# Half of the first block's down projection put off behind the convolution's input products, with its hidden values and split weights kept in DRAM

## The reference

```
# first layer, at its end
h = rms_norm(x, norm_ffn_g)
gp = dwconv_centered(h @ w_ffn_gate, conv_w, conv_b)      # 3 taps over the positions, 2816 channels
x = x + (silu(gp) * (h @ w_ffn_up)) @ w_ffn_down          # the down projection
# second layer, at its start
h = rms_norm_2(x, mix_norm)
a, g = split(h @ a_w_in + a_b_in, 2)                      # two products of 1024 x 1024
u = a * sigmoid(g)
y = causal depthwise convolution of u with 31 taps + conv_b
y = silu(layer_norm(y))                                   # mean and variance over the channels
x = x + y @ a_w_out + a_b_out
x = x + square(relu(rms_norm_2(x) @ w1)) @ w2
```

## Time and profile before

| | |
|---|---|
| median of 3 runs | 3270.68 us (3269.22 to 3271.22) |
| the profiled execution | 3276.46 us, its span 3274.6 us |
| PE busy | 3152.3 us, 96% of the span |
| DVE, ACT, POOL busy | 2012.7, 1067.3, 374.1 us (61%, 33%, 11%) |
| DMA | 288.80 MB, mean 88 GB/s |
| mean granted TensorE clock | 0.982 of full speed |

### The profile page before, as it was taken

How to read it: one execution, slowest core, us unless ns; L and a number is a source line. 1 busy time by engine, 2 the same in 40 slices (tenths; PEclk the granted TensorE clock), 3 DMA queues, 4 the chain that set the end, 5 groups by cost and what they waited for, 6 DMA issues and landing times.

```text
span 3274.6 us, 54823 instructions
## 1 busy us (share of the span) xinstructions
PE 3152.3 (96%) x23414; PEld 2544.0 (78%) x23414; DVE 2012.7 (61%) x3047; ACT 1067.3 (33%) x1528; POOL 374.1 (11%) x354
## 2 busy tenths in 40 slices
PE   8998998899999998999999999999999999999999
PEld 7787886777777777778888888887746888788887
DVE  6665554466766775545444444469979988755544
ACT  5222334445444443222111111132253333433332
POOL 0222441000000000301000000020000000110000
PEclk9999999799999999999999999999999999999999
DMA  3343665122222223421111111111101222223222
GB/s 148 126 135 99 214 213 186 54 75 81 69 86 75 82 81 116 148 90 52 39 52 52 52 42 49 52 39 52 39 13 52 103 91 103 90 90 126 94 91 76
DMA packets 93537, 288.80 MB, mean 88 GB/s; under 512 B 12400, under 2 KB 38640, under 8 KB 72816
## 3 DMA queue, kind: packets, MB, share of 16 engines
q1 hardware_dynamic: 79104, 233.39, 21.1%
q0 software_dynamic: 14192, 51.91, 4.6%
HBM read 228.64 MB, written 56.62 MB: 87 GB/s over the span
## 4 chain that ended last, share of the span: by engine, by line
PE 82%; DVE 10%; ACT 2%; issue 2%; DMA 2%; POOL 1%; SPq 1%; DVEq 0%; ACTq 0%; POOLq 0%
PE ps L2441 24%; PE ps L307 21%; PE ps L489 7%; PE ps L1744 4%; PE ps L2247 3%; PE ps L2603 2%; PE ps L1755 2%; DVE Yh L2630 2%; PE ps L1767 2%; PE ps L2063 1%; PE ps L1387 1%; PE ps L1404 1%; PE ps L1008 1%; PE ps L1398 1%; DVE wlo L287 1%
## 5 line engine op out<-in xcount | busy, mean ns | idle before, releaser
L2441 PE MATMUL ps<-Hh,whi 128*128 128x512 f32 x1600 | 497.6, 392 | 1.3 <-DVE uA L2562 0.7
L283 ACT ACTIVATE whi<-raw 128x2048 fp32r<-128x2048 f32 x139 | 265.5, 1910 | 522.2 <-PE ps L307 296.1
L287 DVE TENSOR_TENSOR wlo<-raw,whi 128x2048 fp32r<-128x2048 f32 x139 | 321.2, 2311 | 95.0 <-ACT whi L283 94.6
L2441 PEld LDWEIGHTS ps<-Hh,whi 128*128 128x128 f32 x1600 | 300.0, 188 | 70.5 <-issue 5.3
L2441 PE MATMUL ps<-Hh,wlo 128*128 128x512 f32 x800 | 311.4, 389 | 0.0
L307 PE MATMUL ps<-Hhi,wlo 128*128 128x512 f32 x672 | 206.9, 389 | 0.0
L307 PE MATMUL ps<-Hlo,whi 128*128 128x512 f32 x672 | 206.9, 389 | 0.0
L307 PE MATMUL ps<-Hhi,whi 128*128 128x512 f32 x672 | 206.8, 389 | 0.0
L2441 PE MATMUL ps<-aHh,whi 128*128 128x512 f32 x512 | 199.5, 390 | 2.7 <-DVE wlo L287 2.5
L2441 PE MATMUL ps<-aLh,whi 128*128 128x512 f32 x512 | 199.2, 389 | 0.0
L2441 PE MATMUL ps<-aHh,wlo 128*128 128x512 f32 x512 | 199.2, 389 | 0.0
(11 more groups left out here) (389 smaller groups left out, 6181.8 us busy)
## 6 DMA issues: line engine op xcount, KB each, us to landing
raw<-in_panels SPq DMA_DIRECT2D x139, 1024.0 KB, 4.8
rwf<-F POOLq DMA_DIRECT2D x16, 1280.0 KB, 6.6
L<-rwf SPq DMA_DIRECT2D x16, 1024.0 KB, 5.0
L<-rwf SPq DMA_DIRECT2D x64, 256.0 KB, 3.5
gts<-so POOLq DMA_DIRECT2D x16, 512.0 KB, 3.5
gl<-gts SPq DMA_DIRECT2D x32, 256.0 KB, 3.6
rwt<-so POOLq DMA_DIRECT2D x15, 512.0 KB, 2.9
qkd<-XTs POOLq DMA_DIRECT2D x16, 384.0 KB, 4.0
```

Of the source, the lines that this page charges most:

```text
L283: e.activation(whi[i % 2][:, :], raw_of(i)[:, :], AF.Copy).then_inc(*a_hi.up(i))
L287: e.tensor_tensor(wlo[i % 2][:, :], raw_of(i)[:, :], whi[i % 2][:, :].bitcast(F32), OP.subtract).then_inc(*v_lo.up(i))
L2441: m = e.matmul(ap, W[wi][:, kc, n0:n0 + 128], mov[mi][:, kc, :], start=x == 0 and q == 0, stop=x == len(kcs) - 1 and q == 2)
```

## The change

**Feed-forward layer.** Only half 0 of the down projection stays in its place (`down_pe`, now 48 matmuls a block, and DVE 8 additions instead of 16). Half 1's rounded part and rest of the hidden values go into `aX` and `aY`, and POOL stores them to DRAM (`hid_pool`, tensors `hdh`, `hdl`). Meanwhile 20 panels are split ahead, the convolution's 8 input panels and 12 panels of the down weights in another cut (`fe`): in 40 pieces of 128 x 1024. POOL loads a piece, ACT rounds it, DVE subtracts, and POOL stores both parts (tensors `sph`, `spl`). There is a single set of buffers for a piece; `sraw` and `slo` are the same memory. So the next load waits until both stores of the piece before have landed. Two pieces go with each channel up to channel 19.

**Convolution.** PE's order is now: half 0's input products, the put-off down projection of half 1 (`rest_pe`, 528 matmuls), half 1's input products, then half 1's taps, `co` and so on. SP loads the split panels back (`pre_sp`, 2 MB each, three sets of buffers) and the hidden values (`hb_sp`). All 248 taps of half 0 are DVE's (`ahead_dve`), two channel tiles in alternation. Half 0's mean and variance sums are formed by POOL (seven additions each), with one product with ones each. POOL's 8 small copies of the 30 positions at the seam (`tail_pool`) go to DVE (`edge_dve`).

```diff
+    def save_load(e, s):
+        i, cols_ = part_s(s)
+        if s:
+            e.wait_ge(*d_ss.by("save", s - 1, "lo"))
+        e.dma_start(sraw[:, :], A["panels"][PIX[SAVED[i]]][:, cols_]).then_inc(*d_sl.up("save", s, "in"))
+    def save_act(e, s):
+        e.wait_ge(*d_sl.by("save", s, "in"))
+        e.activation(shi[:, :], sraw[:, :], AF.Copy).then_inc(*a_ff.up("save", s))
+    def save_dve(e, s):
+        e.wait_ge(*a_ff.by("save", s))
+        e.tensor_tensor(slo[:, :], sraw[:, :], shi[:, :].bitcast(F32), OP.subtract).then_inc(*v_ff.up("save", s))
+    def save_store(e, s):
+        i, cols_ = part_s(s)
+        e.wait_ge(*v_ff.by("save", s))
+        e.dma_start(sph[i][:, cols_], shi[:, :].bitcast(F32)).then_inc(*d_ss.up("save", s, "hi"))
+        e.dma_start(spl[i][:, cols_], slo[:, :].bitcast(F32)).then_inc(*d_ss.up("save", s, "lo"))
...
     def ffn_act(e):
         for blk in range(11):
             for k in range(2):
                 ch = 2 * blk + k
+                if 2 * ch < PIECES_S:
+                    save_act(e, 2 * ch)
                 e.wait_ge(*v_ff.by("c2", ch))
                 e.activation(cv, cv, AF.Silu).then_inc(*a_ff.up("silu", ch))
...
+                if 2 * ch + 1 < PIECES_S:
+                    save_act(e, 2 * ch + 1)
...
     def ffn_pool(e):
         e.wait_ge(*v_h.by(1, "rs"))
+        save_load(e, 0)
         for ch in range(22):
             e.wait_ge(*a_ff.by("silu", ch))
             e.tensor_tensor(cv, cv, rs2, OP.mult).then_inc(*g_ff.up(ch))
+            if ch and ch % 2 == 0:
+                hid_pool(e, ch // 2 - 1)
+            for s in (2 * ch, 2 * ch + 1):
+                if s < PIECES_S:
+                    save_store(e, s)
+                if s + 1 < PIECES_S:
+                    save_load(e, s + 1)
+        hid_pool(e, 10)
...
     def late_pe(e):
         first_pe(e, 0)
+        for ch in range(2, 8):
+            in_pe(e, 0, ch)
+        for g in range(3):
+            rest_pe(e, g)
         first_pe(e, 1)
-        taps_pe(e, 0, 0)
-        for ch in range(2, 8):
-            in_pe(e, ch)
-            taps_pe(e, 0, ch - 1)
-        taps_pe(e, 0, 7)
-        taps_pe(e, 1, 0)
-        mean_pe(e, 0)
-        taps_pe(e, 1, 1)
-        taps_pe(e, 1, 2)
-        var_pe(e, 0)
-        for ch in range(3, 6):
+        for ch in range(2, 6):
+            in_pe(e, 1, ch)
+        added_pe(e, "mu", 0, sy[0])
+        in_pe(e, 1, 6)
+        added_pe(e, "var", 0, sy[1])
+        in_pe(e, 1, 7)
+        for ch in range(4):
             taps_pe(e, 1, ch)
         co_pe(e, 0)
-        taps_pe(e, 1, 6)
+        taps_pe(e, 1, 4)
         last_pe(e, 0)
-        taps_pe(e, 1, 7)
+        for ch in range(5, 8):
+            taps_pe(e, 1, ch)
```

More of the change, by code:

```diff
@@ L2289, in build @@
     rs2 = sb("rs2", 198, [128, S])[:, :]
-    aH = [sb(f"aH{i}", 152 + 16 * i, [128, 2, S], F32R) for i in range(2)]
-    aL = [sb(f"aL{i}", 160 + 16 * i, [128, 2, S], F32R) for i in range(2)]
+    aH = [sb(f"aH{i}", 152 + 8 * i, [128, 2, 512], F32R) for i in range(2)]
+    aL = [sb(f"aL{i}", 156 + 8 * i, [128, 2, 512], F32R) for i in range(2)]
+    aX, aY = sb("aX", 168, [128, 2, 512], F32R), sb("aY", 172, [128, 2, 512], F32R)
+    sraw, slo, shi = sb("sraw", 176, [128, 1024]), sb("slo", 176, [128, 1024], F32R), sb("shi", 180, [128, 1024], F32R)
@@ L2297, in down_pe @@
+    def down_pe(e, b):
+        p = UIX[f"fd{b}"]
         panel_pe(e, p)
         W = weights(p, 2)
-        e.wait_ge(*v.by("lo", b, 1))
+        e.wait_ge(*v_ff.by("lo", b, 1))
         for n in range(8):
[L2301 to L2305, removed]
+            ap, waits = ring.take(("down", b, n), (v_ff, "x", b, n))
+            for w in waits:
+                e.wait_ge(*w)
+            for kc in range(2):
+                for q, (wi, mi) in enumerate(THREE):
+                    m = e.matmul(ap, W[wi][:, kc, 128 * n:128 * n + 128], (aH, aL)[mi][b % 2][:, kc, :],
+                                 start=kc == 0 and q == 0, stop=kc == 1 and q == 2)
+            m.then_inc(*t_ff.up("x", b, n))
+        last_use[p] = (t_ff, ("x", b, 7))
@@ L2306, in down_dve @@
+    def down_dve(e, b):
         for n in range(8):
[L2307 to L2310, removed]
+            e.wait_ge(*t_ff.by("x", b, n))
+            e.tensor_tensor(xT[:, n, hs(0)], ring.bank("down", b, n), xT[:, n, hs(0)], OP.add).then_inc(*v_ff.up("x", b, n))
             if b == 10 and n:
@@ L2470, in added_pe @@
         e.wait_ge(*g_e.by(key, h, 7))
-        e.matmul(ap, ones, sgt[h], start=True, stop=True).then_inc(*t_e.up(key, h, 7))
+        e.matmul(ap, ones, sgt[h] if to is None else to, start=True, stop=True).then_inc(*t_e.up(key, h, 7))
     def sums_pe(e, key, src_by, src, kcs=range(8)):
@@ L2518, in first_pe @@
             e.wait_ge(*w)
[L2519 removed]
+        outs = outs_pe(e, [((x, h, 0), (v_e, x, h, 0), W, n0) for x, n0 in (("a", 0), ("gate", 128))])
         for kc in range(8):
@@ new lines, in in_act, with edge_dve, rest_pe @@
+    def in_act(e, h, ch):
+        e.wait_ge(*v_e.by("gate", h, ch))
+        e.activation(sgt[ch % 2], sgt[ch % 2], AF.Sigmoid, bias=vec("a_b_in", 8 + ch)).then_inc(*a_e.up("sg", h, ch))
+    def edge_dve(e, ch):
+        e.wait_ge(*v_e.by("taps", 0, ch))
+        e.tensor_copy(uB[ch][:, 0:30], uA[ch][:, 512:542]).then_inc(*v_e.up("tail", ch))
+    def rest_pe(e, g):
+        for m_ in range(4):
+            W = pre_pe(e, 8 + 4 * g + m_)
+            if m_ == 0:
+                e.wait_ge(*d_hb.by("hb", g, "hi"))
+                e.wait_ge(*d_hb.by("hb", g, "lo"))
+            for k in range(2):
+                n = 2 * m_ + k
+                half_pe(e, ("x1", g, n), (v_e, "x1", g, n), W, 128 * k, hb[g], range((8, 8, 6)[g]))
@@ L2847, in late_dve @@
     def late_dve(e):
-        done["B"] = 0
+        done["A"] = done["B"] = 0
+        for w in (d_hid.by("hid", 10, "lo"), d_ss.by("save", PIECES_S - 1, "lo")):
+            e.wait_ge(*w)
         for i, u in enumerate(uA):
@@ L3034, in late_sp @@
     def late_sp(e):
-        panels_sp(e, UIX["mg0"] + 7, UIX["mu4'"])
+        panels_sp(e, UIX["mg0"] + 7, CO)
+        for j in range(3):
+            pre_sp(e, j)
+        hb_sp(e, 0)
+        for j in range(3, 28):
+            pre_sp(e, j)
+            if j in (10, 14):
+                hb_sp(e, j // 4 - 1)
+            if j == 24:
+                panel_sp(e, CO)
+        panels_sp(e, CO + 1, UIX["mu4'"])
         for n in range(8):
```

339 lines of the change are left out of this document (193 added, 146 removed).

## The result

The changed kernel takes 3328.73 us, the median of four runs (3325.38 to 3331.86), against 3269.95 (3267.23 to 3271.22) for the kernel before on the same chip: a ratio of 1.0181, 95% interval 1.0163 to 1.0198. It is 58.8 us slower. The forecast was 15 us slower, 3286. The direction and the place were right, the size was not.

What follows compares the result with a forecast made beforehand. PE was taken to bound the kernel, with 82% of the chain. Convolution -54 us and feed-forward layer +69 sum to +15, from 3270.7 to 3286 us; range 3236 to 3330.

Steps and rivals of the forecast that it cites:

- The feed-forward chain: Feed-forward layer: serial piece loads, splits and stores take 57.7 us a block against PE's 54.4; PE waits 3.3 a block.
- the collision term: Feed-forward layer: SP's panel load delays POOL's piece load up to 1.3 us in both channels; wait 4.6 a block.
- The clock: Feed-forward layer: matmuls behind each block's PE wait run slower, costing 2.6 us a block.
- Block 1: Feed-forward layer: block 1's first piece comes late, costing 4 us.
- The convolution: Convolution stage: 65.2 us of PE work saved, old waits of 13.4 gone, new waits of 22.7; sum -54.
- The MLP's first product: Start of the MLP: the old 3.0 us of slow matmuls goes.
- At block 12: MLP: half 1's taps end later, 14 and not 27 being done before the output product; 1.5 us.
- the pieces keep up: Rival, chance 0.20: chain shorter by 4.9 us, nothing waits in the feed-forward layer; 3217 to 3230 us.
- they wait without queueing: Rival, chance 0.20: feed-forward wait comes, but no queueing and hardly a slow matmul; 3251 to 3266 us.
- the loads back bound the convolution: Rival, chance 0.10: at 200 GB/s the convolution stage lasts 335 us, 38 more; 3324 us.
- The estimate by the Trainium skill's page DMA: Bandwidth & Descriptors: Feed-forward layer: pair of stores 4.4, load 3.2, together 7.6 us instead of 8.3; wait about 1.2 a block.
- its case with DMA-bound loads: Convolution: loading panels and hidden values back limits the stage, 38 us more; 3324 us, chance 0.10.

Runs made afterwards that it cites:

- drains-first kernel: Against the changed kernel: in blocks 1 to 9 DVE splits the odd channel's second piece behind the down projection's eight additions, not ahead; 3251.11 us.
- loads-apart kernel: Against the changed kernel: SP's 1 MB panel load waits until POOL's piece load has landed (18 such loads); 3296.09 us.
- One channel later: Pieces on channels 1 to 20, not 0 to 19, against a kernel with drains moved ahead, loads separated, sums on PE, last gate earlier; 3222.88 us.

## Why the prediction was right in kind and wrong in size

- **The feed-forward chain: right.** I had 57.7 us a block without collisions and clock. The block shown has 64.62; without the two loads' excess (2.27 and 2.22) and the gate's (13.79 - 10.88 = 2.9) that is 57.2. Its terms: four stores 6.8, measured 0.54 + 0.53 + 0.52 + 5.39 = 7.0; a pair 4.3, measured 0.53 + 3.76 = 4.3; an undisturbed load 4.0, measured 3.5; ACT's rounding ahead of the silu, and DVE's drains behind the second `slo`, as said. The drains-first kernel shows that this order is what makes the chain PE's.
- **The step that failed is the collision term**, "up to 1.3 each" and "I take 4.6". It was bounded by 1.3 us, since I let the piece share equally with the panel: its own 512 KB once more at 410 GB/s. Measured 2.2 us each in the block shown, 4.5 together, against the 1.3 taken and the 2.6 allowed. Over nine blocks the wait was 67.9 instead of 9 x 4.6 = 41.4: 26.5 us of the 36.5 by which the stage was missed. The loads-apart kernel confirms it: no excess, nine waits of 35.7 us in all (4.0 each, where I had 3.3 without collisions), and 35.0 us of the stage back.
- **The clock: right.** 2.6 a block, 23.4 in all; 23.5 by the means of the page, and 2.9 at the gate of the block shown.
- **Block 1: too small.** I gave it 4 us, for "its first piece comes late". Measured 4.2 + 7.6 = 11.8. I had overlooked that block 0 has four pieces beside 43.5 us of products, since no down projection stands in it. One channel later, the stage is 12.3 shorter. This is 7.8 us of the miss. With the wait and the clock this makes 67.9 + 11.8 + 23.5 = 103.2 of 105.5.
- **The convolution: waits right, what lies behind them not.** -45.5 instead of -52.5 from T to M. The sum on POOL for the mean came at 282.4 behind T (forecast 282), that for the variance at 301.1 (298.5), half 1's first tap at 323.2 (319.9). I had priced DVE's and POOL's instructions as if they didn't meet, and beside each other DVE's eight subtractions took 3.3 us more. Then PE waited 1.16 for a further diagonal matrix, and 2.4 ahead of the last three tiles' taps (idle with ACT as releaser), neither of which I had. These explain 3.3 + 1.2 + 2.4 = 6.9 of 7.0. At block 12 half 1's sum was 4.0 late instead of 1.5. The MLP's first product is free of slow matmuls, as said (10.9 instead of 13.88).
- **The rivals.** That the pieces keep up, and that they wait without queueing, fall by the first line of the waits. That the loads back bound the convolution falls too: PE's waits there are the three above, and none is released by a DMA. The estimate by the Trainium skill's page DMA: Bandwidth & Descriptors was 7.6 us for a pair and a load; measured 0.53 + 3.76 + 0.28 + 3.48 = 8.05, between it and my 8.3.
- **The whole.** On the spans +53.5 instead of +15: 36.5 in the feed-forward layer and 9.3 behind it too little foreseen (7.0 to M and 2.3 behind M), 7.3 less in the stretch ahead. The forecast's range (3236 to 3330) held the time at its upper edge, and its case with DMA-bound loads gave 3324 for another reason: that is luck, not reasoning.

## What to carry to other kernels

A serial chain of small transfers costs little where nobody asks for it in each round: look in every engine's list for what stands behind the wait, and put the drains that PE needs ahead of it (76 to 78 us here, by moving one instruction). Where a transfer is issued just behind a larger one on another queue, allow for the larger one's whole length: equal shares were too little here (1.3 us allowed, 2.2 measured), for one pair of sizes, the only one tried. Before work moves from PE to POOL, check that the sum's wait is not as long as the products it saves, and spread added work by the length of each round, not by their number.

## What the runs showed of the hardware

- A 512 KB load on POOL's queue took 3.5 us alone and 5.7 us when it was issued 0.25 to 1.2 us behind a 1 MB load on SP's queue. 2.2 us more is 0.9 MB at the 410 GB/s of the earlier trace rows: nearly all of the other transfer. The 1 MB load lost nothing (landed at 4.7 and 4.8 us, before at 4.7 to 5.0). By the Trainium skill, DMA: Bandwidth & Descriptors, section Queues, rings and completion order, each engine takes turns between its queues packet by packet. Equal shares of the time, as I read that, would make it 1.3 us, and the measurement decides against them. Into what packets the two loads were cut no run shows, so this doesn't contradict the page; why the piece had all of the delay stays open.
- VectorE's eight 128 x 512 subtractions of two SBUF tiles took 4.91 us alone and 8.20 beside GpSimd's additions. It is not that each was slower: five took 0.68 to 0.69 us, and the three that began while an addition was running took 1.78 and ended 0.55 us behind its end. Two of the three (changed kernel):

```profile
2443.59 1.54 POOL L2569 TENSOR_TENSOR sy<-tl,tl 128x512 f32<-128x512 f32 x1 [6.90 <-ACT tl L2764]
2443.90 1.78 DVE L2757 TENSOR_TENSOR Yh<-Yh,rsh 128x512 f32<-128x512 f32 x1
...
2447.51 1.63 POOL L2569 TENSOR_TENSOR sy<-sy,tl 128x512 f32<-128x512 f32 x1
2447.91 1.78 DVE L2757 TENSOR_TENSOR Yh<-Yh,rsh 128x512 f32<-128x512 f32 x1
```

  By the Trainium skill, SBUF — State Buffer, section SBUF: two separate sides, an instruction of GpSimd and one of VectorE with two SBUF inputs exclude each other on a port pair that they share, and the one that comes second waits for the whole of the first. The trace agrees; I had not priced it. The copy of 128 x 30, which has one SBUF input, took 1.27 instead of 0.17 and also ended just behind an addition (2450.88, the addition 2450.83); the sentence on two inputs doesn't cover it.
- In the block shown, two stores of 512 KB issued one behind the other landed 4.3 us after the first issue and four 7.0, so each further one cost 1.3 to 1.4.
- The stretch ahead of the feed-forward layer, where no edit here puts or moves an instruction, varied by 5.7 us (1443.2 to 1448.9) over the profiles of the ten kernels. Differences of a few us between medians are therefore read from the stage and not from the total.
